# SSD and LRU tiles evicted straight into alternating slots of one buffer, without a DRAM round trip

## What is computed

```python
u = xn @ w['cd_w_in'][j]
z, xbc, dt_in, z_lru, x_lru = _split(u, CD_SIZES)
xbc, sconv_new = _causal_conv(xbc, st_sconv, w['ssd_conv_w'][j], w['ssd_conv_b'][j])
xs, bm, cm = _split(jax.nn.silu(xbc), (SSD_W, SSD_GROUPS * SSD_STATE, SSD_GROUPS * SSD_STATE))
...
y, ssd_new = _scalar_decay(cm, bm, xs * dt[..., None], g, st_ssd)
y = y + w['ssd_d'][j][:, None] * xs
y = (y.reshape(B_, L, SSD_W) * jax.nn.silu(z)).reshape(B_, L, SSD_GROUPS, SSD_W // SSD_GROUPS)
...
xc, lconv_new = _causal_conv(x_lru, st_lconv, w['lru_conv_w'][j], w['lru_conv_b'][j])
r, i = ...                       # sigmoids of block-diagonal products of xc
a = jnp.exp(-LRU_C * r * softplus(-lambda)); b = jnp.sqrt(1 - a * a) * (i * xc)
_, hs = lax.associative_scan(_lin_combine, (a, b), axis=1)
y_lru = hs * jax.nn.silu(z_lru)
y = jnp.concatenate([y_ssd, y_lru], axis=-1) @ w['cd_w_out'][j]
```

## Time and profile before

| | |
|---|---|
| time, median of 3 runs | 2558.11 us (2557.02 to 2559.59) |
| the profiled execution: its time | 2557.48 us |
| the profiled execution: its span | 2555.7 us |
| mean granted TensorE clock | 0.986 of full speed |

### The profile page before, as it was taken

How to read it: one execution, slowest core, us unless ns; L and a number is a source line. 1 busy time by engine, 2 the same in 40 slices (tenths; PEclk the granted TensorE clock), 3 DMA queues, 4 the chain that set the end, 5 groups by cost and what they waited for, 6 DMA issues and landing times.

```text
span 2555.7 us, 52677 instructions
## 1 busy us (share of the span) xinstructions
PE 2445.7 (96%) x22783; PEld 2308.7 (90%) x22783; DVE 1253.8 (49%) x2299; ACT 952.5 (37%) x1531; POOL 382.6 (15%) x590
## 2 busy tenths in 40 slices
PE   7999999999999999999999999999999979999996
PEld 6998888888889999889999999988899979999996
DVE  6644554545544654622343455556655562243332
ACT  5423443234433443432342253333344552243222
POOL 3101111010100101111111111222212111111111
PEclk8999999999999999999999999999999989999998
DMA  9333333333343543643233333333344445223221
GB/s 237 98 96 99 107 93 104 91 94 95 106 118 97 154 141 101 195 164 92 87 90 111 106 109 93 110 110 113 107 122 119 143 152 170 84 82 100 79 85 72
DMA packets 382712, 289.13 MB, mean 113 GB/s; under 512 B 25444, under 2 KB 347758, under 8 KB 381969
## 3 DMA queue, kind: packets, MB, share of 16 engines
q1 hardware_dynamic: 341424, 172.53, 24.9%
q0 software_dynamic: 24640, 81.69, 10.1%
q10 hardware_dynamic: 16416, 31.55, 3.4%
HBM read 229.15 MB, written 57.28 MB: 112 GB/s over the span
## 4 chain that ended last, share of the span: by engine, by line
PE 83%; DVE 5%; ACT 4%; DMA 4%; issue 2%; POOL 0%; SPq 0%; ACTq 0%; DVEq 0%; POOLq 0%
PE psd L562 67%; PE psw L585 2%; PE psw L584 2%; PE psw L605 1%; PE psw L655 1%; PE psw L590 1%; DMA raws<-uT_scratch 1%; PE psw L633 1%; DMA w_raw<-in_ab_w_in_dram 1%; DMA uT_scratch<-mix 1%; PE psw L641 1%; DVE arena L1926 1%; DMA mix<-in_x_prompt_dram 1%; PE psw L627 1%; DMA yT_scratch<-extra 1%
## 5 line engine op out<-in xcount | busy, mean ns | idle before, releaser
L562 PE MATMUL psd<-xh,w_hi 128*128 128x272 f32 x5056 | 1110.7, 301 | 27.7 <-DVE xl L1718 15.4
L562 PE MATMUL psd<-xh,w_lo 128*128 128x272 f32 x5056 | 1051.6, 290 | 0.0
L562 PE MATMUL psd<-xl,w_hi 128*128 128x272 f32 x5056 | 1049.8, 289 | 0.1
L562 PEld LDWEIGHTS psd<-xh,w_hi 128*128 128x128 f32 x5056 | 800.3, 190 | 83.9 <-issue 42.9
L562 PEld LDWEIGHTS psd<-xl,w_hi 128*128 128x128 f32 x5056 | 800.6, 190 | 0.0
L562 PEld LDWEIGHTS psd<-xh,w_lo 128*128 128x128 f32 x5056 | 796.7, 190 | 0.2 <-issue 0.2
L1664 DVE TENSOR_TENSOR w_lo<-w_raw,w_hi 128x512 fp32r<-128x512 f32 x632 | 437.7, 708 | 416.0 <-ACT w_hi L1121 415.0
L1121 ACT CAST w_hi<-w_raw 128x512 fp32r<-128x512 f32 x632 | 377.9, 615 | 671.6 <-PE psd L562 565.2
L2519 POOL TENSOR_TENSOR states<-states,extra 128x544 f32<-128x544 f32 x59 | 80.0, 1356 | 524.8 <-ACT extra L1176 524.8
L2453 POOL DMA_DIRECT2D raws<-uT_scratch x59 | 36.5, 619 | 635.9 <-DMA uT_scratch<-mix 541.6
L2332 DVE TENSOR_TENSOR extra<-psd,rstd 128x544 f32<-128x544 f32 x32 | 23.2, 724 | 156.2 <-PE psd L562 139.2
(11 more groups left out here) (510 smaller groups left out, 2320.7 us busy)
## 6 DMA issues: line engine op xcount, KB each, us to landing
w_raw<-in_ab_w_in_dram SPq DMA_DIRECT2D x224, 256.0 KB, 3.0
w_raw<-in_cd_w_in_dram SPq DMA_DIRECT2D x148, 256.0 KB, 3.2
w_raw<-in_ple_w_gate_dram SPq DMA_DIRECT2D x128, 256.0 KB, 3.1
uT_scratch<-mix ACTq DMA_DIRECT2D x85, 272.0 KB, 2.5
w_raw<-in_ab_w_out_dram SPq DMA_DIRECT2D x64, 256.0 KB, 2.9
w_raw<-in_cd_w_out_dram SPq DMA_DIRECT2D x64, 256.0 KB, 3.0
raws<-uT_scratch POOLq DMA_DIRECT2D x40, 272.0 KB, 3.2
hT_scratch<-arena POOLq DMA_DIRECT2D x8, 1088.0 KB, 10.7
```

The costliest lines, as they stand in the source:

```text
L562: mm = pe.matmul(out[:, D0 + HALF * half:D0 + HALF * (half + 1)], w[:, r, k % QH, :], x[:, k, HALF * half:HALF * (half + 1)], start=(k == ...
```

## The change

All x and z tiles of SSD and LRU go straight from PSUM into `raws`: unit m (SSD 0 to 7, then LRU 0 to 7) has slots 0 and 1 where m is even, 2 and 3 where it is odd. The store, the load and their semaphores are gone for these 32 tiles; readers wait for the eviction itself (`evicted`). VectorE waits before it evicts an x tile until GpSimd has counted the tails of the unit two before (`x_read`). The squares of SSD, which lay in slots 2 and 3, go to `stage`. LEAD is 6 slices less for SSD and 4 to 8 less for LRU, and group r comes 3 instead of 8 slices behind the unit's start (10 as before for LRU 0). With that the table puts r of the LRU units 26, 17, 16, 15, 14, 13, 13 and 13 slices behind the end of their x tile, where it was 32, 28, 26, 24, 22, 22, 22 and 22; all groups of an SSD unit move by 6 slices and keep their distances. Around the start of out1, VectorE and ScalarE do the y tiles, the last eviction and the last gate in another order. A y store of an LRU unit waits for the stores before it.

```diff
-        "ssd": lambda p: 36 - 2 * p, "lru": lambda j: (22, 20, 18, 16, 14, 14, 14, 14)[j]}
+        "ssd": lambda p: 30 - 2 * p, "lru": lambda j: (16, 14, 13, 12, 11, 10, 10, 10)[j]}
...
+        CD = [("ssd", p) for p in range(SSD_H // 2)] + [("lru", j) for j in range(LRU_W // P)]
+        for m, u in enumerate(CD):
+            DIRECT[RAW[u, "x"][0]] = 2 * (m % 2)
+            DIRECT[RAW[u, "z"][0]] = 2 * (m % 2) + 1
+
+        def raw_tile(u, part="x", i=0):
+            at = DIRECT[RAW[u, part][i]]
+            return raws[:, T * at:T * at + T]
+
+        def evicted(u, part="x", i=0):
+            d = RAW[u, part][i]
+            return S[f"dense_read{d % 2}"], d // 2 + 1
...
-                    at_r = last + (10 if u[1] == 0 else 8)
+                    at_r = last + (10 if u[1] == 0 else 3)
...
-                        mm = all_tokens(W, ones[:, :], raws[:, T * (2 + e):T * (3 + e)], start=e == 0, stop=e == 1)
+                        mm = all_tokens(W, ones[:, :], stage[:, e, :], start=e == 0, stop=e == 1)
...
-                act.wait_ge(S["z_loaded"], zloads[u])
-                act.activation(raws[:, T:2 * T], raws[:, T:2 * T], ACT.Silu).then_inc(S["sp_z"], 1)
+                act.wait_ge(*evicted(u, "z"))
+                act.activation(raw_tile(u, "z"), raw_tile(u, "z"), ACT.Silu).then_inc(S["cd_z"], 1)
...
-                    act.wait_ge(S["z_loaded"], zloads["lru", n])
-                    act.activation(lru_z(n), lru_z(n), ACT.Silu).then_inc(S["lr_z"], 1)
+                    fill(SL * (RAW[("lru", n), "z"][0] + 1) + 2)
+                    act.wait_ge(*evicted(("lru", n), "z"))
+                    act.activation(raw_tile(("lru", n), "z"), raw_tile(("lru", n), "z"), ACT.Silu).then_inc(S["cd_z"], 1)
 
                 if u == LAST[1]:
                     gate_of(j - 1)
-                    y_parts(1, 11)
-                    fill(first_slice("out1") + 4)
+                    y_parts(1, 6)
+                    fill(first_slice("out1") + 2)
+                    y_parts(1, 9)
                     gate_of(j)
                     y_parts(1, KT - 2)
...
+                    u, part = TILES[d][4], TILES[d][5]
+                    if u in CD:
+                        m = CD.index(u)
+                        assert m < 2 or (CD[m - 2], part) in used
+                        if part == "x":
+                            dve.wait_ge(S["x_read"], max(1, m))
...
-                    dve.wait_ge(S["u_loaded"], loads["ssd", n])
+                    used.add((("ssd", n), "x"))
+                    fill(SL * (RAW[("ssd", n), "x"][0] + 1) + 2)
+                    dve.wait_ge(*evicted(("ssd", n)))
                     if n > 1:
                         dve.wait_ge(S["sp_y"], n - 1)
                     conv((0,), lambda i, w: pvc("ssd_conv_w", 12 * w + n), lambda i: pvc("ssd_conv_b", n),
-                         lambda i: ssd_x(n), smp_of["ssd", n], S["sp_conv"])
+                         lambda i: ssd_x(n), smp_of["ssd", n], S["sp_conv"], src=2 * (n % 2))
...
-                    dve.wait_ge(S["lr_z"], n + 1)
-                    dve.tensor_tensor(lru_slot(n, 1), lru_slot(n, 6), lru_z(n), ALU.mult).then_inc(S["lr_y"], 1)
+                    fill(SL * (RAW[("lru", n), "z"][0] + 1) + 2)
+                    dve.wait_ge(S["cd_z"], SSD_H // 2 + n + 1)
+                    dve.tensor_tensor(lru_slot(n, 1), lru_slot(n, 6), raw_tile(("lru", n), "z"), ALU.mult).then_inc(S["lr_y"], 1)
+                    used.add((("lru", n), "z"))
 
                 if u == LAST[1]:
                     gated(j - 1)
+                    y_parts(1, 6)
+                    fill(first_slice("out1") + 2)
                     y_parts(1, 11)
-                    fill(first_slice("out1") + 4)
+                    gated(j)
                     y_parts(1, KT - 2)
-                    gated(j)
                 elif not x_first:
...
-                        tails(x, tile(i))
-
-            def tails(x, tile):
+                        tails(x, tile(i), 1 if u[0] in ("bc", "ssd") and i == n - 1 else 0)
+
+            def tails(x, tile, last):
                 link(pool.tensor_copy(hist[:, tile, 0:3], x[:, SEQ - 3:SEQ]))
-                link(pool.tensor_copy(hist[:, tile, 3:27].rearrange("p (b r) -> p b r", b=NB),
-                                      x[:, SEQ:T].rearrange("p (b s) -> p b s", b=NB)[:, :, 1:]))
+                ins = pool.tensor_copy(hist[:, tile, 3:27].rearrange("p (b r) -> p b r", b=NB),
+                                       x[:, SEQ:T].rearrange("p (b s) -> p b s", b=NB)[:, :, 1:])
+                if last:
+                    reads[0] += 1
+                    ins.then_inc(S["x_read"], 1)
...
-                    load_raws(u)
                     sample_rows(u, 1, lambda i: 24)
-                load_raws(u, "z")
                 for base in (0, 32):
...
-                    load_raws(("ssd", p + 1))
-                    sample_rows(("ssd", p + 1), 1, lambda i: 24 + p + 1)
+                    sample_rows(("ssd", p + 1), 1, lambda i: 24 + p + 1, src=2 * ((p + 1) % 2))
                 else:
-                    load_raws(("lru", 0))
                     sample_rows(("lru", 0), 1, lambda i: 36)
...
-                x_first = x_before_z(j)
-                if j and u != LAST[1]:
-                    pool.wait_ge(S["lr_y"], j)
-                if not x_first and u != LAST[1]:
-                    load_raws(u, "z")
                 if j + 1 < LRU_W // P:
                     pool.wait_ge(S["lr_conv"], j + 1)
-                    load_raws(nxt)
-                    sample_rows(("lru", j + 1), 1, lambda i: 36 + j + 1, src=2 * ((j + 1) % 2))
+                    sample_rows(nxt, 1, lambda i: 36 + j + 1, src=2 * ((j + 1) % 2))
                     pool.wait_ge(S["lr_r"], j + 1)
                     load_blocks(j + 1)
-                if x_first:
-                    load_raws(u, "z")
-                    pool.wait_ge(S["z_loaded"], zloads[u])
-                    load_raws(nxt, "z")
                 pool.wait_ge(S["lr_y"], j + 1)
-                x, hs = raws[:, 2 * T * (j % 2):2 * T * (j % 2) + T], lru_slot(j, 6)
-                tails(x, 36 + j)
+                hs = lru_slot(j, 6)
+                tails(raw_tile(u), 36 + j, 1)
                 link(pool.tensor_copy(hist[:, 36 + j, 27:28], hs[:, SEQ - 1:SEQ]))
                 link(pool.tensor_copy(hist[:, 36 + j, 28:36], hs[:, SEQ:T].rearrange("p (b i) -> p b i", b=NB)[:, :, LS - 1]))
                 if j < LRU_W // P - 2:
+                    pool.wait_ge(S["out_stored"], stored[u])
```

More of the change, by code:

```diff
@@ L183 @@
 SEMS = """w_landed0 w_landed1 w_landed2 w_landed3 w_landed4 w_landed5 hi_ready lo_ready slice_done dense_read0 dense_read1 stage_stored0 stage_stored1
-act_chain dve_chain pool_chain work_ready in_copied nrm_sq nrm_ln nrm_rstd x_hi x_ready y_done h_loaded0 h_loaded1 h_loaded2 h_loaded3 z_loaded dn_z gl_z sp_z sq_added sq_summed
+act_chain dve_chain pool_chain work_ready in_copied nrm_sq nrm_ln nrm_rstd x_hi x_ready y_done h_loaded0 h_loaded1 h_loaded2 h_loaded3 z_loaded dn_z gl_z cd_z x_read sq_added sq_summed
 consts_loaded params_loaded rows_loaded xy_loaded0 xy_loaded1 xy_loaded2 xy_loaded3 xy_loaded4 xy_loaded5 h_stored
@@ L293, in trunk @@
         for u in UNITS + UNITS_CD:
-            if u[0] in ("dn", "gla", "ssd", "lru"):
+            if u[0] in ("dn", "gla"):
                 n += 16
@@ L424, in x_before_z @@
             return (("lru", j + 1), "x") in RAW and RAW[("lru", j + 1), "x"] < RAW[("lru", j), "z"]
-        def lru_z(j):
-            at = 3 if ("lru", j) == LAST[1] else 1
-            return raws[:, T * at:T * at + T]
         def y_source(layer, k):
@@ L1647, in _ @@
         def _(dve):
[L1648 removed]
+            at, chained, evac, split, used = [0], [0], [0], [0, 0], set()
             def go(ins):
@@ L2243, in conv_x @@
                 def conv_x(n):
-                    dve.wait_ge(S["u_loaded"], loads["lru", n])
+                    used.add((("lru", n), "x"))
+                    fill(SL * (RAW[("lru", n), "x"][0] + 1) + 2)
+                    dve.wait_ge(*evicted(("lru", n)))
                     conv((0,), lambda i, w: pvc("lru_conv_w", 8 * w + n), lambda i: pvc("lru_conv_b", n),
@@ L2432, in _ @@
         def _(pool):
-            chained = [0]
+            chained, reads = [0], [0]
             def link(ins):
@@ L2443, in load_raws @@
                 n, at = len(tiles), sum(len(RAW.get((u, p), [])) for p in "xvz"["xvz".index(part)::-1][1:])
-                if u[0] == "lru" and part == "x":
-                    at = 2 * (u[1] % 2)
-                if u == LAST[1] and part == "z":
-                    at = 3
                 for e in range(2):
@@ L2473, in sample_rows @@
                 for i in range(n):
-                    x = raws[:, T * i:T * i + T]
+                    x = raws[:, T * (src + i):T * (src + i) + T]
                     if tile(i) < 36:
-                        tails(x, tile(i))
-            def tails(x, tile):
```

(9 more changed lines are left out.)

14 lines of the change are left out of this document (6 added, 8 removed).

## The result

The changed kernel takes **2533.5 us** (median of four runs, 2527.6 to 2535.7) where the kernel before took 2557.6 us beside it (2556.5 to 2559.6): a ratio of 0.991, 95% interval [0.989, 0.993]. In a second set of runs it took 2529.1 us against 2554.6, ratio 0.990 [0.988, 0.991]. The forecast was 2538.5 us with a range of 2531 to 2547; the median lies in that range and under the 2535 to 2542 that the forecast gave as its own. L numbers from here on are those of the kernel that a row comes from; for the changed one, L570 is a dense matmul, L592 a group, L1673 w_lo, L1698 the eviction, L1733 xl, L2648 selp.

What follows compares the result with a forecast made beforehand. TensorE, busy 96% of the span, was taken as the bound, so only its waits and low clock could shrink. Gains of 14.0 + 3.7 + 1.7 = 19.4 us off 2557.5 gave 2538.5 us after a 0.6 us median adjustment, range 2531 to 2547.

Steps and rivals of the forecast that it cites:

- The way into out1: From cd's last tile into out1: cost falls from 20.4 to 6.4 us, with short waits at slices 4 and 6; gain 14.0.
- T: Start of TensorE's group i of unit 7, from which the forecast counts times into out1; slice 0 due at T + 10.7.
- LRU groups: Waits of LRU groups for convolutions or gate matrices: of 4.3 us, 0.5 to 0.6 stay, at unit 1; gain 3.7 us.
- selp: SSD units 2, 4 and 6: GpSimd's z load issue, 0.57 us, leaves the path to selp three times; gain 1.7 us.
- The clock: TensorE at the lower clock after short waits on the way into out1: none to four slices (2.4 us), 0.5 taken.
- rival B: Selp waits lose 1.3 us each as the pair's store lands sooner, and the clock stays up: 2533 us; chance 0.14.
- A: Out1's y tiles become bound by their loads, slice 13 3.9 us later: 2544 us, or 2547 with slower landings; chance 0.18.
- C: VectorE's x evictions in LRU units wait for GpSimd to count tails, giving 24 us back: 2562 us; chance 0.04.
- D: Something the z trip only hid holds the way into out1, slices losing some 20 us: 2553 to 2558 us; chance 0.04.

Runs made afterwards that it cites:

- e0: The changed kernel run again without any edit, beside other runs on one chip: 2529.1 us against 2554.6 for the kernel before.
- e5: The changed kernel with the weight quarters of out1's first tile split into earlier gaps of ScalarE and VectorE: 2529.1 us against 2554.6 for the kernel before.
- e1: The changed kernel with the groups at their old places, keeping direct eviction and the new order around out1: 2537.0 us, ratio 0.992 to the kernel before.
- e3: The changed kernel with the old order of VectorE and ScalarE work around out1: 2534.0 us, ratio 0.991 to the kernel before.
- e9: The kernel before with ScalarE's silu of z of unit 7 moved behind all fourteen loaded y tiles: 2553.3 us, ratio 0.998.
- e2: The kernel before with the new LEAD alone, r still eight slices on, tiles still stored and loaded: 2570.2 us, ratio 1.006.
- e7: The kernel before with selp for units 2, 4 and 6 made ahead of the pair's y store: 2545.0 us, ratio 0.994.
- e8: The changed kernel with the first of selp's two copies done three times, making selp later: 2537.2 us, ratio 0.991 to the kernel before.

## Why the prediction was right, and where its sizes were off

**The way into out1: right.** 14.0 us forecast, 15.1 measured. Every place named came: no wait at slice 0, none at slice 11, one at slice 4 put down to w_lo, one at slice 6. The waits were shorter, 2.2 instead of 3.5 and 1.2 instead of 2, since xl tiles 4 and 5 ended at T + 15.3 and not T + 16.5. I had taken that distance over from the earlier trace rows; but in the earlier trace rows the cast of y tile 3 starts at T + 9.7, behind a load, and in the changed kernel it starts at T + 8.5, behind an xl. And the lower clock, to which I gave 0.5 us, did not come in this trace; in e0's it came and cost nothing in sum. e5 shows that VectorE's queue sets the time of slices 4 and 6. By e1 against before, both at the old places, direct eviction with the new order gives 48.1 - 38.5 = 9.6 of the 15.1 us; the closer places give the other 5.5. By e3 the new order is worth 2.1 at the new places. e9 shows that the trip of z need not cost 8.7 us: with ScalarE's silu behind the y tiles, one wait of 3.0 is left of it, and this one step already gives 5.2 us without direct eviction.

**LRU groups: right in size.** 3.7 us forecast; the 4.3 us of waits are gone. The 0.5 us at unit 1 did not come: the chain worked out as 14.2 us against a slack of 13.7 was too long by at least that. That the tiles are closer bought nothing here (e1: 514.5 against 514.2); e2 shows why it had to be done with the trip removed.

**selp: the right step, mis-sized.** 1.7 us forecast; the waits fell from 9.4 to 6.5, that is 2.9. GpSimd's issue of the z load (0.57 us) is gone from all three, and that is about what the first two gained (2.53 to 2.04, 2.91 to 2.24). GpSimd at unit 2, after (before: the earlier trace rows):

```profile
1684.76 0.73 POOL L2685 DMA_DIRECT2D yT_scratch<-extra  x1 [16.53 <-DVE extra L2252]
1689.57 0.63 POOL L2648 CAST selp<-ident 16x128 fp32r<-16x128 f32 x2 [4.08 <-DMA yT_scratch<-extra]
```

The third (3.95 to 2.24) gained 1.1 us more, because the store itself was issued earlier, 3.56 us ahead of the moment at which TensorE wanted the group in place of 2.45 (1821.00 against 1824.56; 1825.43 against 1827.88). In the trace of before GpSimd came late there: it issued the store 1.67 us after VectorE's last write of the pair had ended (1823.76), against 0.55 us in the changed kernel, with "issue" named as the reason, which says that the trace shows none. e7, which keeps the loads, has the same 1.67 us. Whether the DMA issues that left GpSimd's queue did it, no run shows.

**The clock: counted at nothing, 3.4 us.** This is the largest error. The prediction's sum costed a shorter wait by its length alone, except on the way into out1; only rival B reckoned with the clock behind the selp waits. Behind two of these three waits of before TensorE ran at 1.2 GHz for 3.4 us; behind none of the changed kernel's. e7 gives the same 3.4 us back in the kernel before, and e8 loses some of it again by lengthening the waits. The amount is that of this pair of traces: e9 leaves this stretch of the kernel before as it is, and its trace has the lower clock behind one wait only, so that 1.7 us would be the gain from there.

**The sum.** Forecast 14.0 + 3.7 + 1.7 = 19.4 us; measured in the stage 15.1 + 3.9 (LRU waits of 4.3, less the new 0.4 at L649 in an SSD unit) + 2.9 + 3.4 = 25.3 of 26.3, with 1.0 us not put to a name. The median came out 5.0 us under the forecast, which by its own addition was 2538.7 (2538.1 and 0.6). Way in, LRU groups and selp were right in kind and short by 1.1, 0.6 and 1.2 us; the clock was missing. That the range held the result is owed to the room it left for rival B. The second set's median of 2529.1 lies under it, beside a kernel before that was 3 us lower too.

**The rivals.** *A*, y tiles bound by their loads: not at slices 4 and 6, where e5 won what the queue alone allows, and no row of waits from slice 7 to 13. But the one at slice 12 (0.75 us; 0.9 in e0) is a load's. VectorE waited 1.04 us there for the cast, and ScalarE for the load:

```profile
2082.17 0.65 ACT L1196 CAST xh<-extra 128x544 fp32r<-128x544 f32 x1 [1.89 <-DMA extra<-yT_scratch]
```

So A's mechanism was there, at under 1 us in place of its 5.8. *B*, selp waits shrink further: its time (2533) was met and only half its mechanism. The clock stayed up, but by the median the store landed no sooner. The list of DMA issues of the changed kernel (before: the earlier trace rows):

```profile
extra<-yT_scratch ACTq DMA_DIRECT2D x10, 272.0 KB, 3.0
yT_scratch<-extra POOLq DMA_DIRECT2D x4, 544.0 KB, 4.9
```

The pair's store took 4.9 us by the median, 4.6 before, and the waits stayed above the 2 us that B named (2.04 to 2.24). The 3.3 us that the prediction worked out as an estimate from the Trainium skill, "DMA: Bandwidth & Descriptors", anatomy of one DMA, was not reached by the three stores that selp waits behind (4.8, 5.0 and 5.0 us), although the DMA share while they were under way was 0.54 to 0.57 in place of 0.69 to 0.80. The fourth store landed in 3.2 us, and in e2 the third did so at a share of 0.76; so the share alone does not decide it, and what does is open. The y loads into extra landed in 3.0 us by the median, 3.8 before; those into mix in 4.0, 4.2 before. *C*, evictions that wait for GpSimd: none. *D*, that nothing is gained: no.

## What to carry to other kernels

- When an engine's queue does one thing late, look for the operation that stands in front of it for no reason of its own: three matrices that did not depend on a store waited for it, and moving two small copies ahead of the store was worth 7 us in the stage, against 26 for this large change.
- Taking a trip through DRAM away was worth 20.5 us with every consumer at its old place (e1, with the new order), 9.6 of it at the last tile of the phase. It then lets the consumers move closer, for another 5.8 us; moving them closer without taking the trip away costs more than it wins (e2).
- Price a wait on the matrix engine with what follows it: its length, and then whether the rows behind it show the lower clock.
